# Second block of a two-block network: linear attention merged first, the convolution second, gate chains staggered by tile

## The reference, cut to what matters

```python
def conv_module(val, glu, gate, dw_w, dw_b, ln_g, ln_b, w_o):      # branch 0
    u = val * jax.nn.sigmoid(glu)
    u = lax.conv_general_dilated(u, dw_w[:, None, :], ...) + dw_b     # 31 taps, per channel, 512 channels
    u = jax.nn.silu(layer_norm_2(u, ln_g, ln_b)) * jax.nn.silu(gate)
    return u @ w_o
# branch 1, gated linear attention (4 heads, dk 64, dv 128), forwards and backwards, chunks of 64 tokens
    cum = jnp.cumsum(log_a, axis=2)
    q_in, k_in = q * jnp.exp(cum), k * jnp.exp(-cum)
    o_intra = where(mask, q_in k_in^T, 0) v
    k_state = k * jnp.exp(last - cum);  contrib = k_state^T v
    s = decay * s + contrib                       # from chunk to chunk, context first
    o = o_intra + q_in s_prev;  y = (rms_norm(o, g) * silu(gate)) @ w_o
# branch 2: attention, 8 heads; context attends to context, x to both; y = (o * silu(gate)) @ w_o
    def merge(p, ya, yb, yc):
        return (jax.nn.sigmoid(p[13]) * ya + jax.nn.sigmoid(p[14]) * yb
                + jax.nn.sigmoid(p[15]) * yc) @ w_out
    xs = xs + gate_x[:, None] * merge(px, ya_x, yb_x, yc_x)
```

## Time and profile before

| | |
|---|---|
| median of 3 runs | 1590.02 us (1583.07 to 1592.56) |
| profiled execution | 1596.35 us, span of its instructions 1595.0 us |
| mean granted TensorE clock | 0.931 of 2.4 GHz |
| second block's projections | from about 534 us; layer 0 to 1130, layer 1 from 1186 |

### The profile page before, as it was taken

One profiled execution on the slowest core, in us unless ns is written; L12 is line 12 of the kernel. 1 busy time (PEld: TensorE's weight loads), 2 busy tenths in 40 slices (PEclk: granted clock), 3 DMA queues, 4 the chain that ended last, 5 costly groups with the idle time before them and its releaser, 6 DMA issues.

```text
span 1595.0 us, 18051 instructions
## 1 busy us (share of the span) xinstructions
PE 1411.4 (88%) x6986; PEld 1093.8 (69%) x6986; DVE 907.9 (57%) x1520; ACT 686.1 (43%) x1060; POOL 270.2 (17%) x224
## 2 busy tenths in 40 slices
PE   6998788998795699587999999999989977899998
PEld 5876576876573588464767677778778865666776
DVE  5776567776547429985253333332568954554454
ACT  5444545444535233244322453533454356345453
POOL 0200102200103201221251001011131022320022
PEclk9999997999876799787999999999999977998999
DMA  8532357532345122110111111122353321232253
GB/s 312 171 106 80 114 174 253 170 107 80 110 152 167 40 80 82 54 53 27 54 53 53 54 53 53 54 92 85 102 171 124 118 67 56 90 106 67 79 175 102
DMA packets 48045, 165.13 MB, mean 104 GB/s; under 512 B 5742, under 2 KB 6958, under 8 KB 47704
## 3 DMA queue, kind: packets, MB, share of 16 engines
q1 hardware_dynamic: 47960, 163.98, 31.3%
HBM read 162.91 MB, written 1.05 MB: 103 GB/s over the span
## 4 chain that ended last, share of the span: by engine, by line
PE 58%; issue 17%; DVE 12%; ACT 6%; POOL 4%; DMA 2%; SPq 0%; ACTq 0%; POOLq 0%; DVEq 0%
PE bank L1104 13%; PE bank L1106 12%; PE bank L1105 12%; DVE w_lo L1849 3%; PE bank L1017 3%; PE bank L1388 3%; PE bank L1412 2%; DVE merged L2163 2%; PE bank L1122 2%; PE bank L1123 2%; PE bank L1124 2%; ACT w_hi L1453 1%; DMA w_raw<-in_w 1%; PE bank L1351 1%; PE bank L1357 1%
## 5 line engine op out<-in xcount | busy, mean ns | idle before, releaser
L1849 DVE TENSOR_TENSOR w_lo<-w_raw,w_hi 128x1024 fp32r<-128x1024 f32 (+3 forms) x304 | 375.1, 1241 | 250.6 <-ACT w_hi L1453 250.3
L1453 ACT ACTIVATE w_hi<-w_raw 128x1024 fp32r<-128x1024 f32 (+3 forms) x304 | 312.3, 1032 | 369.7 <-PE bank L1106 206.0
L1104 PE MATMUL bank<-w_hi,x_hi 128*128 128x512 f32 (+3 forms) x1072 | 453.0, 423 | 1.2 <-DVE x_lo L1859 1.2
L1106 PE MATMUL bank<-w_hi,x_lo 128*128 128x512 f32 (+3 forms) x1072 | 417.4, 389 | 0.0
L1105 PE MATMUL bank<-w_lo,x_hi 128*128 128x512 f32 (+3 forms) x1072 | 416.5, 389 | 0.0
L1104 PEld LDWEIGHTS bank<-w_hi,x_hi 128*128 128x128 f32 x1072 | 208.3, 194 | 52.0 <-issue 17.1
L1106 PEld LDWEIGHTS bank<-w_hi,x_lo 128*128 128x128 f32 x1072 | 206.5, 193 | 42.3
L1105 PEld LDWEIGHTS bank<-w_lo,x_hi 128*128 128x128 f32 x1072 | 208.0, 194 | 33.0 <-issue 0.2
L2163 DVE SCALAR_TENSOR_TENSOR merged<-conv_u,par,merged 128x512 f32<-128x512 f32 (+1 forms) x240 | 136.0, 629 | 0.1
L1036 PE MATMUL bank<-w_hi,mod_c_cut 128*128 128x512 f32 x96 | 47.7, 497 | 36.9 <-DVE w_lo L1849 36.9
L2495 POOL TENSOR_TENSOR merged<-merged,sigma 128x512 f32<-128x512 f32 x24 | 33.3, 1407 | 270.2 <-DVE sigma L2207 270.0
(11 more groups left out here) (339 smaller groups left out, 1977.1 us busy)
## 6 DMA issues: line engine op xcount, KB each, us to landing
w_raw<-in_w SPq DMA_DIRECT2D x168, 512.0 KB, 3.5
w_raw<-in_wm SPq DMA_DIRECT2D x48, 512.0 KB, 3.5
w_raw<-in_wo SPq DMA_DIRECT2D x40, 512.0 KB, 3.6
w_raw<-in_wy_conv SPq DMA_DIRECT2D x8, 512.0 KB, 3.4
w_raw<-in_wy_gla SPq DMA_DIRECT2D x8, 512.0 KB, 3.4
w_raw<-in_wy_att SPq DMA_DIRECT2D x8, 512.0 KB, 3.5
w_raw<-in_w SPq DMA_DIRECT2D x8, 460.0 KB, 6.6
par<-in_small SPq DMA_DIRECT2D x2, 1218.0 KB, 8.6
```

Source lines behind the costliest of these rows:

```text
L1104: mm(out, xh[:, q, col], hi[:, kk, 0:w], start=q == 0 and kind != "in2", stop=False)
L1106: ins = mm(out, xl[:, q, col], hi[:, kk, 0:w], start=False, stop=last and kk == KP - 1)
L1453: do(hi, raw, ACT.Copy).then_inc(sem["cut_hi"], 1)
L1849: v.tensor_tensor(lo, raw, hi.bitcast(F32), ALU.subtract).then_inc(sem["cut_lo"], 1)
```

## The change

`BRANCHES` gives each layer's order of branches: in layer 0 linear attention, convolution, attention; in layer 1 convolution, linear attention, attention. The chunks are reordered accordingly: layer 0 is KKV, LRQ, GV, VAL, GLU, AQ, GG, then M1A, y1, M1B, y1, then CGATE, M0A, y0, M0B, y0, then AG, M2A, y2, M2B, y2; layer 1 is VAL, GLU, KKV, LRQ, GV, AQ, CGATE, M0A, y0, M0B, y0, GG, M1A, y1, M1B, y1, AG and the rest. The first branch of a layer is written to `merged`, the others are added.

The convolution gets `conv_val` and `conv_u` of its own; its gate `cg` takes the place of `conv_u` after the last tap, GLU's sigmoid that of `att_q`. The outputs of the silu of GG (and in layer 1 of AG) are kept in `merged` instead of passing through `gate_tmp`, and `gated` becomes a step of its own after `gla_n` (`att_out2`). The taps lie between the end of GLU and 6 positions after the start of M1B (layer 1: of AQ). The scan begins at GV (layer 0: before VAL and GLU), is laid out as a pipeline over the tiles in stages decays, sums, turned, products, and has two buffers for la, e1, e2, four for the gate sums and a separate `k_t`. The turning of a branch's input goes after every second projection step instead of every third.

The diff, cut to its core:

```diff
-SIGMA = {M0A: (0, 0), M0B: (0, 1), M1A: (1, 0), M1B: (1, 1), M2A: (2, 0), M2B: (2, 1)}
+MERGE = [(M0A, M0B), (M1A, M1B), (M2A, M2B)]
+
+BRANCHES = [(1, 0, 2), (0, 1, 2)]
...
+def gates_kept(l, c):
+
+    return l == LAYERS - 1 or c == GG
+
+
 def gated(l, c, t):
-    return [("ev_gate", l, c, t), ("gated", l, c, t)]
+    return [("ev_gate", l, c, t)] + ([] if gates_kept(l, c) else [("gated", l, c, t)])
 
 
...
     cut = lambda i: (flip(f"y{i}", l, t, 0) for t in tiles)
-    for c in FIRST_CHUNKS[l]:
-        if c == KKV:
-            for t in EVERY:
-                yield ("need", ("mi_lo", l, t, 4))
-            yield from inp(KKV, EVERY, evacuate2)
+    context = [("need", ("mi_lo", l, t, 4)) for t in EVERY]
+    if l == 0:
+        yield from context
+        yield from inp(KKV, EVERY, evacuate2)
+        yield from inp(LRQ, EVERY, evacuate2)
+        yield from inp(GV, EVERY, evacuate2)
+        yield from project_t(l, VAL)
+        yield from project_t(l, GLU)
+        yield from inp(AQ, tiles, evacuate2)
+        yield from inp(GG, tiles, gated)
+    else:
+        yield from project_t(l, VAL)
+        yield from project_t(l, GLU)
+        yield from context
+        yield from inp(KKV, EVERY, evacuate2)
+        yield from inp(LRQ, EVERY, evacuate2)
+        yield from inp(GV, EVERY, evacuate2)
+        yield from inp(AQ, tiles, evacuate2)
+    for i in BRANCHES[l]:
+        first, second = MERGE[i]
+        if i == 0:
+            yield ("need", ("tap", l, TAPS - 1, 3))
+            yield from project_t(l, CGATE)
+            yield from inp(first, tiles, sigma)
+            yield ("need", ("conv_lo", l, 3))
+        elif i == 1:
+            if l == LAYERS - 1:
+                yield from inp(GG, tiles, gated)
+            for t in tiles:
+                yield ("need", ("gla_n", l, t))
+            yield [("gated", l, GG, t) for t in tiles]
+            yield from beside(inp(first, tiles, sigma), cut(i), 2)
         else:
-            yield from project_t(l, c)
-    yield from inp(LRQ, EVERY, evacuate2)
-    yield from inp(GV, EVERY, evacuate2)
-    yield from project_t(l, CGATE)
-    yield from inp(M0A, tiles, sigma)
-    yield ("need", ("conv_lo", l, 3))
-    yield from inp(AQ, tiles, evacuate2)
-    yield from y(0, 0)
-    yield from inp(M0B, tiles, sigma)
-    yield from y(0, 1)
-    for t in tiles:
-        yield ("need", ("gla_n", l, t))
-    yield from inp(GG, tiles, gated)
-    yield from beside(inp(M1A, tiles, sigma), cut(1), 3)
-    yield from y(1, 0)
-    yield from inp(M1B, tiles, sigma)
-    yield from y(1, 1)
-    for t in tiles:
-        yield ("need", ("att_out2", l, t))
-    yield from inp(AG, tiles, gated)
-    yield from beside(inp(M2A, tiles, sigma), cut(2), 3)
-    yield from y(2, 0)
-    yield from inp(M2B, tiles, sigma)
-    yield from y(2, 1)
+            if not gates_kept(l, AG):
+                for t in tiles:
+                    yield ("need", ("att_out2", l, t))
+            yield from inp(AG, tiles, gated)
+            if gates_kept(l, AG):
+                for t in tiles:
+                    yield ("need", ("att_out2", l, t))
+                    yield [("gated", l, AG, t)]
+            yield from beside(inp(first, tiles, sigma), cut(i), 2)
+        yield from y(i, 0)
+        yield from inp(second, tiles, sigma)
+        yield from y(i, 1)
 
...
+    if branch_before(l, 0) is not None:
+        yield ("need", ("project", f"y{branch_before(l, 0)}", l, 1, 1, tiles_of(l)[-1]))
...
 def gla(l):
     tiles = tiles_of(l)
-    for c in (KKV, GV, LRQ):
+    for c in (KKV, LRQ):
         for t in EVERY:
             yield ("need", ("ev2", l, c, t))
     yield [("gla_zero", l), ("gla_one", l), ("w_up", l), ("lr_flip", l), ("lr_t", l)]
-    for s in (1, 0):
-        some = C_TILES if s else X_TILES
-        shown = some[0] in tiles
-        for t in some:
-            yield [("gla_z", l, t), ("gla_e", l, t), ("gla_la", l, t)]
-            yield [("gla_left", l, t), ("gla_e3", l, t), ("gla_ks", l, t)]
-            yield [("gla_tot", l, t), ("gla_dec", l, t)]
-            if shown:
-                yield [("gla_cum", l, t), ("gla_e12", l, t), ("gla_qi", l, t), ("gla_ki", l, t)]
-                yield [("gla_qf", l, t), ("gla_qt", l, t)]
-                yield [("gla_kf", l, t), ("gla_kt", l, t)]
-                for par in range(2):
-                    yield [("gla_a", l, t, par), ("gla_m", l, t, par)]
+
+    def decays(t):
+        yield [("gla_z", l, t), ("gla_e", l, t), ("gla_la", l, t)]
+
+    def sums(t):
+        yield [("gla_left", l, t), ("gla_e3", l, t), ("gla_ks", l, t)]
+        yield [("gla_tot", l, t), ("gla_dec", l, t)]
+        if t in tiles:
+            yield [("gla_cum", l, t), ("gla_e12", l, t), ("gla_qi", l, t), ("gla_ki", l, t)]
+
+    def turned(t):
+        if t in tiles:
+            yield [("gla_qf", l, t), ("gla_qt", l, t)]
+            yield [("gla_kf", l, t), ("gla_kt", l, t)]
+
+    def products(t):
+        if t in tiles:
+            for par in range(2):
+                yield [("gla_a", l, t, par), ("gla_m", l, t, par)]
+
+    def states(s):
         for i in range(4):
             yield [("gla_con", l, s, i, d) for d in range(2)] + [("gla_st", l, s, i, d) for d in range(2)]
-        if shown:
-            for t in some:
-                yield [("gla_o", l, t), ("gla_o1", l, t), ("gla_o2", l, t)]
-                yield [("gla_sq", l, t), ("gla_ms", l, t), ("gla_iv", l, t), ("gla_n", l, t)]
-        if s == 1:
-            yield [("gla_cp", l)]
+
+    def outputs(t):
+        if t in tiles:
+            yield [("gla_o", l, t), ("gla_o1", l, t), ("gla_o2", l, t)]
+            yield [("gla_sq", l, t), ("gla_ms", l, t), ("gla_iv", l, t), ("gla_n", l, t)]
+    yield from pipeline(C_TILES, [decays, sums, turned, products], [0, 1, 2, 3])
+    for t in EVERY:
+        yield ("need", ("ev2", l, GV, t))
+    yield from states(1)
+    yield from beside(pipeline(X_TILES, [decays, sums], [0, 1]), (g for t in C_TILES for g in outputs(t)), 2)
+    yield [("gla_cp", l)]
+    yield from pipeline(X_TILES, [turned, products], [0, 1])
+    yield from states(0)
+    for t in X_TILES:
+        yield from outputs(t)
...
-        cg = p.at["project_t", l, CGATE, 0, 0]
-        y = p.at["project", "y0", l, 0, 0, 0]
+        at_y = lambda i: p.at["project", f"y{i}", l, 0, 0, 0]
         if l > 0:
             p.side(modulated(l, C_TILES), p.at["project_t", l, VAL, 0, 0] - 2, p.at["project_t", l, GLU, 2, 0])
-        p.side(conv(l), p.at["project_t", l, GLU, 3, 3] + 1, at(AQ) - 8)
-        p.side(conv_end(l), at(AQ) - 7, at(AQ) - 1)
-        p.side(key_heads(l), cg, at(AQ))
-        p.side(gla(l), cg + 2, at(GG) - 2)
-        p.side(query_heads(l), y, y + 12)
-        p.side(attention(l), at(GG) + 4, at(AG) - 2)
+        glu = p.at["project_t", l, GLU, 3, 3]
+        if l == 0:
+            p.side(gla(l), at(GV), at_y(1) - 6)
+            p.side(conv(l), glu + 1, at(M1B) + 6)
+            p.side(conv_end(l), p.at["project_t", l, CGATE, 1, 0], at_y(0) - 1)
+            p.side(key_heads(l), glu + 4, at(AQ))
+            p.side(query_heads(l), at(AQ) + 6, at(M1A))
+            p.side(attention(l), at_y(1), at(AG) - 2)
+        else:
+            p.side(conv(l), glu + 1, at(AQ) + 6)
+            p.side(conv_end(l), p.at["project_t", l, CGATE, 0, 3], at_y(0) - 1)
+            p.side(key_heads(l), at(GV), at(AQ))
+            p.side(query_heads(l), at(AQ) + 6, at(M0A))
+            p.side(gla(l), at(GV), at(GG) + 2)
+            p.side(attention(l), at(GG) + 3, at(M2A))
...
-        b.cv, b.u2 = (b.acc[:, i:i + 2, :].rearrange("p a (b t) -> p (a b) t", t=2 * S) for i in (0, 2))
+        b.cv, b.u = sb("conv_val", [P, 4, 2 * S]), sb("conv_u", [P, 4, 2, S + 2 * PAD])
+        b.cg = b.u[:, :, :, :].rearrange("p c s t -> p (c s t)")[:, 0:4 * 2 * S].rearrange("p (c t) -> p c t", c=4)
...
-            b.la, b.e1, b.e2 = (sb(n, [P, 512], F32, scope) for n in ("gla_la", "gla_e1", "gla_e2"))
-            b.e3, b.q_t = sb("gla_k_state", [P, 2, 512], F32, scope), sb("gla_q_t", [P, 4, 2, P], F32, scope)
-            b.k_t, b.dec = b.la, sb("gla_decay", [P, 4, 4], F32, scope)
+            b.la, b.e1, b.e2 = (sb(n, [P, 2, 512], F32, scope) for n in ("gla_la", "gla_e1", "gla_e2"))
+            b.e3, b.q_t = sb("gla_k_state", [P, 4, 512], F32, scope), sb("gla_q_t", [P, 4, 2, P], F32, scope)
+            b.k_t, b.dec = sb("gla_k_t", [P, 512], F32, scope), sb("gla_decay", [P, 4, 8], F32, scope)
...
+            squares = sb("conv_squares", [P, 4, 2 * S], F32, scope)
+            high, low = (sb(n, [P, 4, 2 * S], F32R, scope, "right") for n in ("y_hi", "y_lo"))
...
+        b.y = [(high, low), (b.xh[:, 0:4, S:2 * S], b.xl[:, 0:4, S:2 * S])]
+        b.u2 = [squares, b.cv[:, :, S:2 * S]]
...
-            act.wait_ge("conv_g", l, 3)
+            act.wait_ge("conv_u", l, 3)
...
-        act.wait_ge("conv_u", l, j)
+        act.wait_ge("tap", l, TAPS - 1, 3)
...
+        if gates_kept(l, c):
```

(13 more changed lines are left out.)

179 lines of the change are left out of this document (92 added, 87 removed).

## The result

| | before | after |
|---|---|---|
| median of 4 runs each, same chip | 1588.28 us (1583.07 to 1592.56) | 1568.80 us (1565.27 to 1569.50) |
| ratio after to before | | 0.9855, 95% interval 0.9823 to 0.9888 |
| profiled execution | 1596.35 us, span 1595.0 | 1569.50 us, span 1568.1 |

The account below looks back on a forecast made before the run. VectorE was taken to bound layer 0's tap stretch, with TensorE elsewhere slowed by waits on the scan and gate weights. Gains of 20 us in layer 0 and 35 in layer 1 gave 1590 - 55 = 1535 us, range 1498 to 1572.

Parts of the forecast that it names:

- rival (3): GpSimd excludes the taps in full: layer 0's tap stretch 204 us, layer 0 loses 9, layer 1 gains 25; 1574 us, chance 0.12.
- w_up: Sign in layer 0: TensorE's 13.5 us wait on the gate weights goes, no such wait above 3 us.
- VectorE's share in B: Sign: VectorE above 90% busy from layer 0's first tap to the last, some 175 us; below 70% means wrong.
- the wait before M1A: Sign that the forecast is wrong: a long wait before M1A in layer 0, from the scan's tail.
- B = 163/0.93 = 175: Layer 0, GLU's end to 6 units into M1B: 163 us of VectorE work with 7% idle, 175 us; bounds 153 and 204.
- The tail costs nothing extra: Layer 0: projections wait for the scan's last groups before M1A, at no extra time, since VectorE has taps to do.
- A = 124: Layer 0, KKV to GLU: projections 99 us, scan's TensorE work 20, first tile's chain 5, together 124 us.
- C, D, E, F: Layer 0 after the taps: M1B's rest, y1 38 us; CGATE, M0A 75, conv_end 4; y0, M0B 67.5; AG to y2 92.
- Layer 1: Taps' stretch 95 us against 90, taps' end to GG's end 88 against 128: gain 35 us, bounds 20 and 50.
- (5): Rival: scan round trips and in-order queues entangle VectorE and TensorE; VectorE 56% busy, tap stretch 273 us, 1633 us, chance 0.07.
- (2): Rival: the chains vanish altogether, layer 0 gains 42 us and layer 1 50, giving 1498 us; chance 0.22.
- (4): Rival: taps gain no room, staggering the scan saves nothing, only the w_up wait goes; 1576 us, chance 0.06.

Follow-up runs that it names:

- e5: Kernel after, but layer 0's 120 taps behind the first of each chunk take only 256 of 512 columns (second stream's convolution not computed): 1553.2 us.
- e2: Kernel after with layer 0's key heads asked for from GV + 2 until ahead of GLU's last unit, instead of between GLU and AQ: 1569.6 us.
- e6: Kernel after with GpSimd multiplying by the gain before it waits for the sum of squares, the small power behind that wait: 1563.6 us.
- e9: Kernel after with layer 0's query heads moved from AQ + 6 .. M1A to M1A .. y1 + 2, attention starting 2 units later: 1573.3 us.
- e13: Kernel after with M1A's 16 units in layer 0 emitted before the stop for gla_n instead of behind it: 1560.8 us.
- e1: Kernel after with layer 0's scan asked to end 8 units behind GG's start instead of 6 units ahead of y1: 1574.1 us.
- e8: Kernel after with layer 1's query heads between the first y0 piece and GG instead of between AQ + 6 and M0A: 1556.3 us.
- e4: Kernel after with the scan emitted tile after tile in both layers, as before, and waiting for all of GV at its start: 1593.6 us.
- e16: Kernel after with the scan tile after tile, waiting for all of GV, in layer 0 alone: 1578.6 us.
- e15: Kernel after with e13, e6 and e8 together, plus layer 0's VAL and GLU ahead of GV, scan and key heads from VAL on: 1545.9 us.

## Why the prediction was wrong

The sign and most stretches held; the size didn't: 20 to 27 us where 55 were forecast. That 1568.8 lies inside the recorded range is due to the range's upper end, which half of rival (3) set; the sum behind the forecast failed. (The chances add up to 0.81 and 0.12 where the text has 0.82 and 0.11.) Of the signs named, w_up, the clock behind B and layer 1's waits on la (6.8 us) came out as forecast; VectorE's share in B (77.5%, not 90) did not, and the wait before M1A appeared.

**The step that failed most is B = 163/0.93 = 175.** The work came out 11 us below the 163: 151.9, of which the taps' 92.5 are 6.4 over the earlier trace rows where 10 were forecast for GpSimd beside them (57.2 us of it, 61 forecast). The 7% of idle time is what failed: 12 us were allowed and 44 measured, 22.5%, nearly all of it VectorE waiting for GpSimd, ScalarE and TensorE. It came from a stretch before with little else in VectorE's queue, while B now holds all heads and half of a scan, whose steps go from VectorE to GpSimd or TensorE and back. e5 shows that VectorE's work still counts 0.69 us per us; e2, e6, e9 and e13 found no single hole behind the rest: 4.5, 2.0, 2.3 and 6.2 us of A + B. The trace named the higher share too: the upper bound, 204 at 80%, from layer 1's taps in the earlier trace rows, was the nearer row.

**"The tail costs nothing extra" failed in its reason.** A pause before M1A was to appear only if VectorE weren't full. It appeared with VectorE idle for 20.5 us from 767 to 821, because the plan emits side steps by position: the taps due beside M1A stood before the stop in VectorE's queue. Moving M1A into it gave back not the 31 us that the gap shows but 6.2 (e13).

**A = 124 was 134.9.** Beside its 99 us of projections it had 20 us for the scan's TensorE work, sized by the spacing of projection matmuls, and a chain of 5. The waits were 3.1 us, the rest 33: the 30 steps of the scan there are recorded at 28.3 us and the bias matmuls, which the unit of 1.36 us leaves out, at 4.6. By the recorded 64.6 us, the upper bound, 27 of 50 groups are 35, so the scale 0.227/0.39 didn't hold for these small matmuls. Five more steps in A cost 17.6 us (e1): 11.3 of recorded work and 5.8 of waits.

**C, D, E, F:** 33, 74, 67 and 93 against 38, 79, 67.5 and 92. The 4 us for conv_end weren't needed. With A 11 and B 21 above, and C and D 10 below, the sum is 597 against 575.5: layer 0's gain of 20 is gone, and the old order did as well.

**Layer 1:** the taps' stretch was 95, as forecast; taps' end to GG's end 102 instead of 88. e8 names the 14: 10.7 are the query heads in CGATE's place, whose GpSimd round trips hold up gla_la and the convolution's end. That move was priced at nothing. Attention was 86 instead of 93, which gives 7 back; TensorE's busy time there fell from 90.6 to 84.6 us as its clock rose from 0.93 to 1.00. Together 28 us for a forecast of 35.

**What the gain is made of** agrees with the forecast mechanism: chains of the scan that TensorE waits for got other work between their steps, and TensorE's waits on them fell. By e4 the scan's new layout is worth 25 us; e16 puts 10 of them in layer 0, where they don't quite pay for the 13 that the new place costs, and 15 in layer 1, where the rest of the change brings 12 more. How much of the 25 is the staggering and how much the start before GV is complete isn't shown, since e4 takes back both. That the wider place for the taps brings room found no support in e4.

**The rivals.** (3) gives B = 204 and is the nearest in time (1574), but not in cause. By the Trainium skill, page "SBUF — State Buffer", section "Who interferes with whom", taps and GpSimd would exclude each other. The forecast and the rival both charge every us of GpSimd that moves into B, but by the trace only 19.9 of its 57 lie beside a tap. The 24 taps there take 9.7 us more than at the 0.66 us of the other 96, 0.49 us per us beside each other, and GpSimd's instructions get longer too:

```profile
722.24 1.26 POOL L2640 TENSOR_TENSOR att_q<-att_q,rows 128x512 f32<-128x512 f32 x1
732.04 1.57 POOL L2640 TENSOR_TENSOR att_q<-att_q,rows 128x512 f32<-128x512 f32 x1
731.74 3.08 DVE L2242 SCALAR_TENSOR_TENSOR conv_val<-conv_u,par,conv_val 128x512 f32<-128x512 f32 x3
819.65 5.38 DVE L2242 SCALAR_TENSOR_TENSOR conv_val<-conv_u,par,conv_val 128x512 f32<-128x512 f32 x8
```

So the trace agrees that the two hinder each other, and neither shows nor excludes a full lock while both run; the 10 us are far from the rival's 39 (10 in the 163, 29 more). (5), engines entangled by in-order queues, fits the traced waits, at a fifth of its size: VectorE's share was 77.5%, between its 56% and the 93% of the forecast, above its turning point of 66%. (2) is excluded. (4) is right that the taps gain no room, but not that the new scan saves nothing: without it even the w_up gain doesn't show.

**Still open:** how the scan's 25 us divide, why e15's A + B gains 5 us more than its parts, and how much of B's remaining idle time (48 us of 212 in e15) could go: six mixtures moved it about, and the one with 90% paid in A.

## What to carry to other kernels

When steps are moved beside a full engine, take its idle share from the row that holds the same mix of hand-overs, not from the row of the stream alone. A two-step ping-pong between in-order engines costs the engine its wait, and also whatever critical step is queued behind it: put such steps where the engine that sets the end has its own work to do (one line, 10.7 us). Filling a stop of 31 us gave 6, so price a hole by what its work would displace, and try the move before summing holes. Where a planner has stops, look at which side steps it has emitted by then.

## What the runs showed that I had not expected

What GpSimd costs the taps doesn't shrink with them. From 512 to 256 columns in the same place the 120 taps fell from 92.5 to 60.4 us (e5). The taps with no GpSimd instruction beside them stand 0.66 us apart at 512 columns and 0.40 at 256; what the others take over that is 9.7 us in the kernel after and 9.6 in e5. In layer 1 the same 256-wide taps, with 0.7 us of it before and 4.2 after, went from 49.9 to

```profile
L2242 DVE SCALAR_TENSOR_TENSOR conv_val<-conv_u,par,conv_val 128x256 f32<-128x256 f32 x120 | 53.8, 510 | 0.0
```

So halving a tap's columns saves 0.26 us of it, and nothing of what GpSimd beside the taps costs.

A stop in the projections also costs clock. In the 32 us between GG and M1A TensorE was busy 23.9, but with small scan matmuls; its clock was 1.00 up to 768 us and 0.50 from 772 to 796, though it was busy 18.7 of those 24 us. At the other stop TensorE idled from 711 to 732 us; its clock was 0.50 from 716 on and still was for the first 4 us of work behind it.
